# High halves on ScalarE, low halves on VectorE: moving the weight split off GpSimd in a one-core decoder layer

## What is computed

```
mod = silu(c) @ w_ada + b_ada                 # per sequence, six vectors
h   = rms_norm(x) * (1 + sc_a) + sh_a
z   = h @ w_in                                # 1024 -> 7680 columns
q, k, v, rq, rf, ri, rg, ga, gr = split(z)
o_attn = sliding window attention with sinks and ALiBi (16 heads, 4 kv heads)
o_rec  = HGRN2 recurrence (8 heads, 128x128 state), rms_norm, * silu(rg)
x   = x + g_a * ((sig(ga) * o_attn + sig(gr) * o_rec) @ w_out)
h2  = rms_norm(x) * (1 + sc_m) + sh_m
x   = x + g_m * (relu(h2 @ w_up)^2 @ w_down)  # 1024 -> 4096 -> 1024
y   = rms_norm(x)
```

## Time and profile before

| | |
|---|---|
| runs | 1296.21, 1297.41, 1300.94 us; median 1297.41 us |
| span of the profiled execution, first to last instruction | 1294.2 us |
| DVE, ACT, POOL busy | 677.0, 373.6, 534.4 us |
| PE busy, as matmuls overlap | 1200.5 us |
| mean granted clock of PE | 0.954 of full speed |
| high halves on DVE | 66 instructions, 82.2 us |
| low halves on POOL | 256 instructions, 338.1 us |

### The profile page before, as it was taken

One profiled execution on the slowest core, in us unless ns is written; L12 is line 12 of the kernel. 1 busy time (PEld: TensorE's weight loads), 2 busy tenths in 40 slices (PEclk: granted clock), 3 DMA queues, 4 the chain that ended last, 5 costly groups with the idle time before them and its releaser, 6 DMA issues.

```text
span 1294.2 us, 21890 instructions
## 1 busy us (share of the span) xinstructions
PE 1200.5 (93%) x8733; PEld 1128.4 (87%) x8733; DVE 677.0 (52%) x1357; ACT 373.6 (29%) x737; POOL 534.4 (41%) x400
## 2 busy tenths in 40 slices
PE   5799999989989898988997999979999999999996
PEld 4699878878978887978887999969999999999996
DVE  5722356656487656296469444372425435345364
ACT  3400245565324343353332210152010110110114
POOL 1433311100455432354344243546655554655640
PEclk9899999979989988989988999989999999999997
DMA  9778411212313221112211126512232222223112
GB/s 308 215 173 286 135 44 56 66 33 66 123 34 100 68 68 52 50 33 81 87 48 53 52 75 221 155 48 66 66 98 72 93 68 96 75 89 98 66 33 73
DMA packets 121257, 120.45 MB, mean 93 GB/s; under 512 B 19268, under 2 KB 111132, under 8 KB 120869
## 3 DMA queue, kind: packets, MB, share of 16 engines
q1 hardware_dynamic: 121157, 119.06, 29.1%
HBM read 109.22 MB, written 11.80 MB: 94 GB/s over the span
## 4 chain that ended last, share of the span: by engine, by line
PE 75%; DVE 16%; issue 3%; ACT 3%; DMA 1%; POOL 1%; SPq 0%; DVEq 0%; ACTq 0%; POOLq 0%
PE PS L767 52%; PE PS L726 5%; PE PS L882 2%; PE PS L807 2%; DVE qt L1442 2%; DVE kt L1443 2%; PE PS L836 1%; PE PS L717 1%; PE PS L924 1%; PE PS L908 1%; DVE wR L1279 1%; DVE xhat L1255 1%; DVE att L1460 1%; PE PS L931 1%; DVE b L1349 1%
## 5 line engine op out<-in xcount | busy, mean ns | idle before, releaser
L1572 POOL TENSOR_TENSOR wR<-raw,wR 128x512 fp32r<-128x512 f32 x256 | 338.1, 1321 | 525.9 <-DVE wR L1279 509.5
L767 PE MATMUL PS<-hR,wR 128*128 128x288 f32 x3744 | 543.5, 304 | 1.9 <-ACT tmp L1059 1.0
L767 PEld LDWEIGHTS PS<-hR,wR 128*128 128x128 f32 x3744 | 518.5, 194 | 19.2 <-issue 13.9
L767 PE MATMUL PS<-actR,wR 128*128 128x288 f32 x1920 | 257.7, 295 | 2.0 <-DVE actR L1426 1.8
L767 PEld LDWEIGHTS PS<-actR,wR 128*128 128x128 f32 x1920 | 255.1, 188 | 2.4 <-DVE actR L1426 2.0
L1077 ACT ACTIVATE tmp<-PS 128x576 f32<-128x576 f32 x32 | 20.8, 652 | 305.6 <-PE PS L767 302.0
L1337 DVE CAST actR<-tmp 128x576 fp32r<-128x576 f32 x32 | 22.2, 695 | 159.5 <-ACT tmp L1078 159.5
L882 PE MATMUL PS<-qt,kt 128*128 128x64 f32 x448 | 62.5, 285 | 36.0 <-issue 29.6
L882 PEld LDWEIGHTS PS<-qt,kt 128*128 128x128 f32 x448 | 58.6, 202 | 41.3 <-issue 33.6
L1597 POOL TENSOR_TENSOR D<-b 128x512 f32<-128x512 f32 (+1 forms) x56 | 66.9, 1195 | 61.2 <-DVE kt L1443 57.9
L1279 DVE CAST wR<-raw 128x2048 fp32r<-128x2048 f32 x66 | 82.2, 1246 | 16.7 <-PE PS L726 14.5
(11 more groups left out here) (211 smaller groups left out, 1340.5 us busy)
## 6 DMA issues: line engine op xcount, KB each, us to landing
raw<-in_w_in SPq DMA_DIRECT2D x26, 1024.0 KB, 5.3
raw<-in_w_up SPq DMA_DIRECT2D x16, 1024.0 KB, 5.6
raw<-in_w_down SPq DMA_DIRECT2D x16, 1024.0 KB, 5.0
mid<-in_w_ada SPq DMA_DIRECT2D x12, 1024.0 KB, 5.2
ada<-in_w_ada SPq DMA_DIRECT2D x8, 1024.0 KB, 12.3
raw<-in_w_in SPq DMA_DIRECT2D x16, 256.0 KB, 5.7
S<-in_state_hgrn SPq DMA_DIRECT2D x8, 512.0 KB, 4.2
out_hgrn_sample<-S SPq DMA_DIRECT2D x8, 512.0 KB, 4.8
```

Of the source, the lines that this page charges most:

```text
L767: mm = pe.matmul(PS[:, 2 * x.pair + h, 0:HALF], weights(x, w, k, col), rhs[r], start=(k == 0 and n == 0), stop=(k == last and n == 2))
L1572: done(pool.tensor_tensor(w[:, 1, cols], raw[SLOT[SPLITS[n]]][:, cols], w[:, 0, cols].bitcast(F32), ALU.subtract), s_lo)
```

## The change

ACT writes the high half of each unit from the third on, in four quarters, each just ahead of the low quarter in the list. DVE writes the low quarters and waits for `s_hi` at each. POOL splits nothing. `s_hi` now counts four for each unit. The waits for the load and for the buffer stand ahead of ACT's first quarter.

```diff
@@ block.scalar
-            done = ordered(act, s_act)
+            done = ordered(act, s_act, {s_hi: 8})
...
+            def hi(n, q):
+                u = SPLITS[n]
+                if q == 0:
+                    act.wait_ge(s_raw[SLOT[u]], raw_loads(u))
+                    act.wait_ge(s_mm, LAST[SPLITS[n - 2]] + 1)
+                cols = slice(q * UW // 4, (q + 1) * UW // 4)
+                done(act.activation(wR[split_index(n)][:, 0, cols], raw[SLOT[u]][:, cols], ACT.Copy), s_hi)
...
+                elif ev == "lo" and x[0] >= 2:
+                    hi(*x)
@@ block.vector
             def hi(n):
                 u = SPLITS[n]
                 dve.wait_ge(s_raw[SLOT[u]], raw_loads(u))
-                if n >= 2:
-                    dve.wait_ge(s_mm, LAST[SPLITS[n - 2]] + 1)
-                done(dve.tensor_copy(wR[split_index(n)][:, 0, :], raw[SLOT[u]][:]), s_hi)
-
-            def lo(n):
+                done(dve.tensor_copy(wR[split_index(n)][:, 0, :], raw[SLOT[u]][:]), s_hi, 4)
+
+            def lo(n, q):
                 w = wR[split_index(n)]
-                done(dve.tensor_tensor(w[:, 1, :], raw[...][:], w[:, 0, :].bitcast(F32), ALU.subtract), s_lo, 4)
+                if n < 2:
+                    done(dve.tensor_tensor(w[:, 1, :], raw[...][:], w[:, 0, :].bitcast(F32), ALU.subtract), s_lo, 4)
+                    return
+                dve.wait_ge(s_hi, 4 * n + q + 1)
+                cols = slice(q * UW // 4, (q + 1) * UW // 4)
+                done(dve.tensor_tensor(w[:, 1, cols], raw[...][:, cols], w[:, 0, cols].bitcast(F32), ALU.subtract), s_lo)
...
-                elif ev == "hi":
+                elif ev == "hi" and x[0] < 2:
                     hi(*x)
-                elif ev == "lo" and x[0] < 2 and x[1] == 0:
-                    lo(x[0])
+                elif ev == "lo" and (x[0] >= 2 or x[1] == 0):
+                    lo(*x)
@@ block.gpsimd
-            done = ordered(pool, s_pool, {s_lo: 8})
-
-            def lo(n, q):
-                if n < 2:
-                    return
-                pool.wait_ge(s_hi, n + 1)
-                w = wR[split_index(n)]
-                cols = slice(q * UW // 4, (q + 1) * UW // 4)
-                done(pool.tensor_tensor(w[:, 1, cols], raw[...][:, cols], w[:, 0, cols].bitcast(F32), ALU.subtract), s_lo)
+            done = ordered(pool, s_pool)
...
-                if ev == "lo":
-                    lo(*x)
-                elif ev == "norm":
+                if ev == "norm":
```

More of the change, by code:

```diff
@@ L1276, in hi @@
                 dve.wait_ge(s_raw[SLOT[u]], raw_loads(u))
-                if n >= 2:
-                    dve.wait_ge(s_mm, LAST[SPLITS[n - 2]] + 1)
-                done(dve.tensor_copy(wR[split_index(n)][:, 0, :], raw[SLOT[u]][:]), s_hi)
-            def lo(n):
+                done(dve.tensor_copy(wR[split_index(n)][:, 0, :], raw[SLOT[u]][:]), s_hi, 4)
+            def lo(n, q):
                 w = wR[split_index(n)]
-                done(dve.tensor_tensor(w[:, 1, :], raw[SLOT[SPLITS[n]]][:], w[:, 0, :].bitcast(F32), ALU.subtract), s_lo, 4)
+                if n < 2:
+                    done(dve.tensor_tensor(w[:, 1, :], raw[SLOT[SPLITS[n]]][:], w[:, 0, :].bitcast(F32), ALU.subtract), s_lo, 4)
+                    return
+                dve.wait_ge(s_hi, 4 * n + q + 1)
+                cols = slice(q * UW // 4, (q + 1) * UW // 4)
+                done(dve.tensor_tensor(w[:, 1, cols], raw[SLOT[SPLITS[n]]][:, cols], w[:, 0, cols].bitcast(F32), ALU.subtract), s_lo)
             def residual(x, m, gate):
@@ L1563, in _ @@
         def _(pool):
-            done = ordered(pool, s_pool, {s_lo: 8})
-            def lo(n, q):
-                if n < 2:
-                    return
-                pool.wait_ge(s_hi, n + 1)
-                w = wR[split_index(n)]
-                cols = slice(q * UW // 4, (q + 1) * UW // 4)
-                done(pool.tensor_tensor(w[:, 1, cols], raw[SLOT[SPLITS[n]]][:, cols], w[:, 0, cols].bitcast(F32), ALU.subtract), s_lo)
+            done = ordered(pool, s_pool)
             def squares(n, k):
```

## The result

| | before | after |
|---|---|---|
| median of 12 runs each, us | 1295.54 (1288.41 to 1302.7) | 1286.97 (1284.43 to 1289.7) |
| ratio, 95% interval | | 0.9924 [0.9903, 0.9944] |
| span of the profiled execution, us | 1294.2 | 1285.1 |
| mean granted clock of PE | 0.954 | 0.961 |
| DVE, ACT, POOL busy, us | 677.0, 373.6, 534.4 | 732.4, 535.4, 182.6 |

A forecast was written before the change was run, and what follows sets the result against it. PE bounds the MLP; the recurrence's gaps wait for DVE's operands, held by POOL. Span: 1294.2 - 14.4 (recurrence) + 1 (attention) + 1.7 (between projections) = 1282.5 us; the median lies 3.2 higher, 1285.7, given as 1285; range 1271 to 1303.

The forecast's parts named there:

- Rival A: Recurrence: low quarters only change sides and still meet line 1597's differences; half the gains, no clock back; 1295 us, chance 0.26.
- (a): Recurrence, seven slots: the first low quarter replaces the rounding and `kt` shortens, 1.48 us each, 10.2 us gained in all.
- (c): Recurrence, slots with both operands beside POOL's low quarters: two gaps shrink by 2.0 us in sum.
- the 3 us of costs: Recurrence: 1 us for DVE waiting in order for ACT, 2 us for the added second and third quarters on DVE.
- (b): Recurrence, four slots with operands right behind POOL's last quarters: DVE's quarter fits its idle time, gaps shrink by 3.6 us.
- The 4 us for the clock: Recurrence: shorter gaps may save some clock falls; 4 us taken, between bounds of nothing and 11 us.
- a third of the 33 us: Recurrence: upper bound of 11 us for the clock gain, from missing clock worth 33 us of full-speed work.
- rival C: Recurrence: more clock returns if most falls behind the seven gaps go, another 10 us; 1275 us, chance 0.13 (below 1278).
- The sign that I had named for a failure: DVE waits of over 0.5 us for ACT's `wR` many times ahead of operands would show the prediction wrong.
- the loop: Attention: ACT's exponentials and high quarter, DVE's low quarter and maxima form a 4.45 us cycle against PE slots of 3.6 to 4.0.
- up to 1 us in each of three units: Attention: what remains of DVE falling behind, after slack and the removed rounding; 2.5 us lost in all.
- Rival B: Attention's loop reaches 5 us, and the same handshake eats the recurrence's gain; about 1307 us, chance 0.14 with other losses.

The follow-up runs named there:

- p1: The kernel before, but in the recurrence POOL writes two zero memsets for each low quarter and reads nothing; the low product is left out: 1276.93 us.
- p2: The kernel before, but in the recurrence POOL writes three zero memsets for each low quarter; the low product is left out: 1279.32 us.
- e2: The kernel before, but units 13 to 25, those of the recurrence, split as in the change: 1273.36 us.
- e1: The changed kernel, but units 8 to 12, those of attention, split as before: 1282.37 us.
- e4: The changed kernel, but the one unit split between output projection and MLP (up 1) split as before: 1283.17 us.
- b1: The kernel before, but attention units split as changed with ACT one place ahead, and recurrence units split as in the change: 1269.82 us.
- m1: The kernel before, but in the recurrence the high halves move to ACT in quarters while POOL keeps the low halves: 1293.04 us.
- m2: The kernel before, but in the recurrence DVE rounds whole tiles and also subtracts the low quarters; POOL splits nothing: 1292.23 us.
- e3: The kernel before, but only units 8 to 12, those of attention, split as in the change: 1305.19 us.
- m3: The kernel before, but in attention DVE rounds whole tiles and subtracts the low quarters too, without a handshake: 1299.5 us.
- m4: The kernel before, but attention units split as in the change with ACT writing each high quarter one place earlier: 1290.77 us.
- b2: The kernel before, but attention and recurrence units split as in the change with ACT one place ahead in both: 1265.89 us.

## Why the prediction was right in total, step by step

**The mechanism of the recurrence: right.** The operands waited for POOL's low quarters, and stop doing so when POOL no longer reads SBUF beside them: 1308 ns beside a quarter, 443 beside nothing, 443 beside a `memset` (p1; 526 ns long, so that an operand held until its end would have taken some 0.26 us more in the mean) and 440 in p2. What the prediction had read from one `kt`, which ended 0.32 us behind POOL's quarter, the trace before shows at all 62 operands that begin inside an instruction of POOL: they end 0.28 to 0.35 us behind its end. Rival A (1295 us), that POOL would hold the operands as much as before because the differences of line 1597 remain, falls: in p1 they still meet 24 operands and hold them for 1040 ns, and the recurrence gains 19.0 of e2's 21.6 us all the same; in the changed kernel, with other times of DVE, they meet only 9. The gaps shrank by 11.7 us; (a) to (c) at 0.85 less the 3 us of costs had been 10.4. Those before line 882 are at 23.6 us, where I had said about 20. By term, each gap looked up at the same instruction: the seven gaps of (a) fall from 18.3 to 10.5 us (to 0, 1.77, 3.15, 2.74, 1.61, 0 and 1.21), 7.8 where 10.2 had been worked out; the four of (b) by 3.5 for 3.6; the two of (c) by 1.1 for 2.0. "1.48 us each" holds for the work of DVE and not for PE's wait: four of the seven gaps gave back only 0.5 to 0.8 us, the last 2.4. That makes 12.4 for the 13.4 that I counted, and all other gaps together grew by 0.9, for costs of 3.

**The 4 us for the clock: mis-sized.** They were an estimate out of 0 to 11, and no run shows them. The runs showed this in their place: 24.8 less 11.7 leaves 13.1 us that no gap explains, and time at clock 0.50 fell by 30.8 us, worth up to 15.4. With the same split in e1, e2, e4 and b1 it fell by 20.5 to 27.4. The upper bound that I gave, a third of the 33 us, was too low as well. I had argued that a gap of 3.5 us keeps 2 us of its length and therefore its fall. The slot at 563 even kept 2.74, and the clock is 0.50 behind it too, from 568.2 to 575.0 us, but "low" fell by almost half. This is rival C's mechanism, at its size; C's total was not reached because attention took it back. That it is the split in the recurrence, and nothing upstream, is shown by e2. Why the clock comes back with the whole change and hardly with m1 or m2 isn't shown: their gaps are 33 us each, those of e2 25. The sign that I had named for a failure, DVE's long waits for ACT's quarter, is there as well (this row, 358 to 705 us), and mostly harmless here, since PE had work at hand: none of the twelve waits lies beside a gap of PE over 0.25 us, the longest ends at 538.98 us, and PE has no such gap from 505 to 550:

```profile
DVE wR L1298 <- ACT wR L993: 47.7, 12, 10.1
```

**Attention: right loop, wrong price.** I gave the loop 4.45 us and it takes 4.47, and a cost of 2.5 less a gain of 1.6. Measured: +8.5 in the changed kernel, +8.6 in e3. m3 and m4 split it: DVE's own work without a handshake costs nothing that can be told (1.1, where kernels with the old split are at 0.7 to 2.0), and with the handshake eased by one place the stretch gains 3.0. So the gain side was, if anything, small at 1.6, and what the loop costs, taken between e3 and m4, is 8.6 + 3.0 = 11.6 us, not 2.5. The failed step is "up to 1 us in each of three units": I let the slack of 0.99 us and the 0.5 us from the rounding be there again for each unit, and counted only what fell behind beyond them. DVE waited 15 times, for 1.3 us in the mean, three or four times in each of four units (9 to 12), and the table of shifts shows the loss spread over the whole stretch, not over three units. Where ACT had an evacuation (`rv`, 0.38 us) ahead of its quarter a turn took 4.89. Of the 8.5, 5.8 are gaps of PE over 0.25 us (5.9 to 11.7), and at most 0.7 are clock: time at clock 0.50 in the stretch rose from 15.7 to 17.1 us. Rival B had this mechanism in the right place, and was wrong in that it let the recurrence suffer the same.

**Between the projections: right delay, wrong consequence.** The copy `part` was to come 4.4 us later against ACT's square (0.10 us before it). The timelines of DVE and PE after, where the square began at 829.15:

```profile
830.60 2.87 DVE L1298 TENSOR_TENSOR wR<-raw,wR 128x512 fp32r<-128x512 f32 x4 [2.84 <-ACT wR L993]
833.50 0.42 DVE L1252 COPY part<-PS 128x256 f32<-128x256 f32 x1
833.96 0.81 DVE L1258 SCALAR_TENSOR_TENSOR mods<-mods,vec 128x18 f32<-128x18 f32 x4
```
```profile
833.98 0.65 PE L776 MATMUL PS<-collect,part 128*128 128x9 f32 x4 [1.77 <-DVE part L1252]
```

It is 4.35 us behind the square, 4.45 later than before, and the four small instructions take 0.81 us instead of 2.56, near the 0.5 forecast. I then let only 1.7 us come through; 4.9 did, and e4 ties all of it to this unit. The delay itself was right: PE's gaps in the stretch grow by 1.8 us. The rest is clock: it is at 0.50 for 12.9 us there, where it was for 4.4 (the granted clock is 0.65 in the third row of the first fence under "The result"). So each later step of the chain of modulation tiles takes longer too: one step lasts 3.22 us (835.04 to 838.26), with 16 matmuls in 1.93 us, where it lasted 1.95, with 1.07. The step that failed took PE's work behind the wait at its old speed.

**Output projection and MLP: +1.5 and +1.8 for 0.** The quarters hide under PE as forecast, and the idle time of ACT ahead of them is harmless (columns: busy us, mean ns, idle before, of it for PE):

```profile
L993 ACT ACTIVATE wR<-raw 128x512 fp32r<-128x512 f32 x256 | 161.8, 632 | 140.6 <-PE PS L767 132.9
```

Yet 1.8 us of 400 are lost in the MLP, in small pieces. e2, b1 and b2, which split these units as before, lose nothing there, and e4, which doesn't, loses 1.8; so it belongs to these units' split, and no run says by which part.

The +1.5 of the output projection doesn't belong to the split. PE's gaps there are the same 1.8 us before and after, and the trace after has one stretch of 3.4 us at clock 0.50 that the trace before lacks. m1, e3 and m2 split these units as before and have such a stretch and the +1.5 too; e4 splits them anew and has neither. These are m1 and e4, in the columns of the earlier trace rows:

```profile
719.00:801.00 82.00, 80.24 (x594) 80.01 (x593) 38.35 (x46) 10.12 (x15) 32.91 (x24) 0.98 0.32 111
709.00:790.00 81.00, 79.24 (x597) 79.01 (x596) 43.06 (x62) 25.36 (x39) 0.00 (x0) 1.00 0.31 105
```

What brings it about is not shown.

**The sum.** Recurrence 10.4 us better than forecast; attention 7.5, between the projections 3.2, and output projection and MLP 3.3 us worse, against 0.6 won ahead of attention: the errors cancel to 3 us of span. The total was right only because terms that were off by 10.4 and 7.5 us had opposite signs; that is luck.

## What to carry to other kernels

Move the instruction that holds up the operands on the critical path, but only in the stage where these operands are late: 13 of 64 units carried all of the gain (e2), and of the other 51 those of attention, between the projections and of the MLP cost. When work that one engine did alone is cut in two between engines that already wait for each other, lay the two lists side by side and let the producer lead by one place; without it the handshake closes a loop and every slot that is shorter than the loop pays (3.6 to 4.0 us against 4.47; e3 against m4, 14 us of the total). And where shorter stalls are the aim, look at the granted clock of the stretch as well: it gave back here about as much as the gaps themselves (13.1 us and 11.7).

## What the runs showed of the hardware that was not expected

- Where POOL only wrote beside DVE's two-input instructions, it cost them nothing: 128x512 `memset`s of 526 ns, two or three in a row, left `qt` and `kt` at 443 and 440 ns (p1, p2); a `tensor_tensor` of 1292 ns took them to 1308 in the mean (before). The quarters that moved to DVE are held in the same way: 692 ns by themselves, 1945 in the mean for 15 of the MLP that began beside POOL's `actR` (after).
- The clock's share of a stall: the gaps of the recurrence fell by 31% (38.3 to 26.6 us), time at clock 0.50 by 47% (64.9 to 34.1 us). It also varies by itself: with the same split in the recurrence five kernels have gaps of 25.0 to 27.3 us and from 34.1 to 44.4 us at clock 0.50.
